# Modulation weights as row pieces with column-tiled products in the mix-in steps of a hybrid retention and convolution network

## What is computed

```python
def adaln(cond, w_ada, b_ada):
    return jnp.split(jax.nn.silu(cond) @ w_ada + b_ada, 6, axis=-1)

# one layer, latent stream
sh1, sc1, g1, sh2, sc2, g2 = adaln(c, w_ada[l], b_ada[l])
p = modulate(x, sh1, sc1) @ w_in[l]                       # modulate: h * (1 + scale) + shift
q, k, v = ...                                             # 8 heads of 64, rotary q and k
o_f, _ = retention_scan(q, k, v, lg_f, s_f)               # chunks of 128, both directions
o_b, _ = retention_scan(flip_seq(q), flip_seq(k), flip_seq(v), lg_b, s_b)
mix_x = mixer_output(o_f + flip_seq(o_b), p, ..., w_out[l])   # gated retention | conv module
x = layer_norm(DEEPNORM_ALPHA * x + g1 * mix_x, ln1_w[l], ln1_b[l])
x = mlp_sublayer(x, sh2, sc2, g2, w_ff1[l], w_ff2[l], ln2_w[l], ln2_b[l])
```

## Time and profile before

| | us |
|---|---|
| three runs | 3217.91, 3218.61, 3223.07 |
| median | 3218.61 |
| profiled execution, its own time | 3222.41 |
| its span in the trace | 3220.6 |
| TensorE busy, and share of the span | 2902.3, 90% |
| VectorE busy, and share of the span | 2237.7, 69% |

### The profile page before, as it was taken

The page is one execution under the profiler, slowest core; times in us unless marked ns, Lnnn a source line. Parts: engine busy times, 40 slices in busy tenths (PEclk is TensorE's granted clock), DMA queues, the critical chain, the costliest instruction groups (busy, mean ns, idle before and its releaser), DMA issues.

```text
span 3220.6 us, 36797 instructions
## 1 busy us (share of the span) xinstructions
PE 2902.3 (90%) x12840; PEld 2268.5 (70%) x12840; DVE 2237.7 (69%) x3490; ACT 709.3 (22%) x1416; POOL 1036.7 (32%) x939
## 2 busy tenths in 40 slices
PE   7798999778699999999997599998797999999994
PEld 1487778347588888888885487784376787777873
DVE  0497675376777786868688787652667778777787
ACT  0322323332311111111111333332323111111111
POOL 0133435165411111111113444462553222222124
PEclk9898999889899999999999799998898999999997
DMA  9311112443011111111112311114421111111111
GB/s 360 73 40 46 48 36 99 138 146 91 26 40 39 39 39 39 39 36 36 35 37 27 104 41 52 56 56 173 132 82 39 53 44 47 46 45 52 39 46 65
DMA packets 256867, 216.06 MB, mean 67 GB/s; under 512 B 60864, under 2 KB 204800, under 8 KB 256768
## 3 DMA queue, kind: packets, MB, share of 16 engines
q10 hardware_dynamic: 143112, 125.89, 12.7%
q1 hardware_dynamic: 113656, 88.93, 9.1%
HBM read 191.62 MB, written 23.17 MB: 67 GB/s over the span
## 4 chain that ended last, share of the span: by engine, by line
PE 75%; DVE 12%; issue 6%; POOL 3%; ACT 2%; DMA 2%; SPq 0%; ACTq 0%; POOLq 0%; DVEq 0%
PE bank L515 12%; PE bank L517 12%; PE bank L516 12%; PE bank L940 8%; PE bank L941 8%; PE bank L942 8%; PE bank L591 5%; PE bank L815 2%; PE bank L816 2%; PE bank L817 2%; DVE work L1565 2%; PE bank L871 1%; PE bank L870 1%; DVE x_hl L1336 1%; PE bank L854 1%
## 5 line engine op out<-in xcount | busy, mean ns | idle before, releaser
L1301 POOL TENSOR_TENSOR w_lo<-raw,w_hi 128x1024 fp32r<-128x1024 f32 x120 | 305.2, 2544 | 1174.8 <-ACT w_hi L1159 1174.8
L1567 DVE TENSOR_TENSOR work<-work 128x512 f32<-128x512 f32 x576 | 555.2, 964 | 20.0
L515 PE MATMUL bank<-w_hi,h_hi 128*128 128x512 f32 x1152 | 458.3, 398 | 43.4 <-DVE work L1565 43.4
L940 PE MATMUL bank<-x_hl,w_hi 128*128 128x512 f32 (+1 forms) x1280 | 474.8, 371 | 2.7 <-ACT work L1150 1.4
L941 PE MATMUL bank<-x_hl,w_hi 128*128 128x512 f32 (+1 forms) x1280 | 472.8, 369 | 0.0
L942 PE MATMUL bank<-x_hl,w_lo 128*128 128x512 f32 (+1 forms) x1280 | 472.3, 369 | 0.0
L517 PE MATMUL bank<-w_hi,h_lo 128*128 128x512 f32 x1152 | 451.7, 392 | 0.0
L516 PE MATMUL bank<-w_lo,h_hi 128*128 128x512 f32 x1152 | 451.5, 392 | 0.0
L1565 DVE TENSOR_TENSOR work<-bank,work 128x512 f32<-128x512 f32 x576 | 393.1, 682 | 0.0
L1466 DVE SCALAR_TENSOR_TENSOR bank<-work,bank 128x512 f32<-128x512 f32 (+1 forms) x580 | 366.5, 696 | 3.9
L1544 DVE TENSOR_TENSOR work<-work 128x512 f32<-128x512 f32 (+1 forms) x160 | 124.9, 781 | 347.3 <-ACT work L1150 347.3
(11 more groups left out here) (131 smaller groups left out, 4451.9 us busy)
## 6 DMA issues: line engine op xcount, KB each, us to landing
raw<-in_w_ff ACTq DMA_DIRECT2D x128, 512.0 KB
plain_words<-in_w_ada SPq DMA_DIRECT2D x12, 2048.0 KB
plain_words<-in_w_ada ACTq DMA_DIRECT2D x12, 2048.0 KB
raw<-in_w_in ACTq DMA_DIRECT2D x64, 256.0 KB
raw<-in_w_in ACTq DMA_DIRECT2D x16, 512.0 KB
raw<-in_w_out ACTq DMA_DIRECT2D x16, 512.0 KB
gate_rows<-work SPq DMA_DIRECT2D x80, 64.0 KB, 1.6
retention_rows<-work SPq DMA_DIRECT2D x72, 64.0 KB, 1.5
```

Of the source, the lines that this page charges most:

```text
L515: nc.tensor.matmul(out_ps, hi, whi, start=first, stop=False)
L940: nc.tensor.matmul(o, slot(mlp_slot(f), 0)[:, wc], x_hi[:, k, cols], start=k == 0, stop=False)
L1301: nc.gpsimd.tensor_tensor(slot(mlp_slot(sl), 1), raw[:, un % 2, :], slot(mlp_slot(sl), 0).bitcast(F32), ALU.subtract).then_inc(w_ready, 1)
L1567: nc.vector.tensor_tensor(X[:, t, hc], X[:, t, hc], y_t[:, yi % 2, :], ALU.add).then_inc(S["y_add"], 1)
```

## The change

The modulation product is cut by rows as well as by columns. A section is one of the 12 vectors of 1024 columns (6 a layer), a piece is 128 rows of it, 512 KB, and eight pieces make a section. For a piece TensorE does four products of 256 columns each, whose outputs stand at partitions 0, 32, 64 and 96 of one bank, so in four column groups of the array. VectorE adds the bias with four instructions of 2 x 256.

- Only sections 0 and 1 precede the first modulate phase: 16 pieces, loaded by SP in four sets, then the tokens in three loads, then the stores of both rows.
- Sections 2 to 7 go with steps 2 to 49 of layer 0's mix-in, and sections 8 to 11 with steps 2 to 33 of layer 1's, one piece a step, at the end of the step's work. There is one piece buffer: SP loads a piece (two transfers of 256 KB) when the products of the one before are done. A section's first product waits until VectorE has added the bias of the section before (`ada_row`), and VectorE does that in the same step, behind its taps.
- Tail and mix-out have no modulation work, and ScalarE issues none of its loads.
- The section's bank is bank 7 (bank 6 for section 1), so the convolution has bank 3 alone: `conv_chain` now does the two latent runs one after the other, and every tap waits for its direct predecessor.
- The modulate phase of both layers transposes into five banks in place of two; in layer 0 ScalarE loads and splits the first four units of projection weights ahead of it, in place of among its steps. The modulation rows are read back ahead of the decay rates.

```diff
-ADA_FIRST, ADA_TAIL = 12, 6
-ADA_LATE = 2
+ADA_FIRST = 2
+ADA_SECTIONS = [list(range(ADA_FIRST, 6 + ADA_FIRST)), list(range(6 + ADA_FIRST, 12))]
+ADA_PIECES_FIRST = ADA_FIRST * KT
...
-    return [(tap, lat + r) for tap in range(TAPS) for r in range(2)] + [(tap, r) for r in range(lat) for tap in range(TAPS)]
+    return [(tap, r) for r in (*range(lat, lat + 2), *range(lat)) for tap in range(TAPS)]
...
             plan.append(("taps", ct, a, b))
             if b < len(chain):
                 taps.insert(0, (ct, b))
+        if stored:
+            plan.append(("ada_bias", stored.pop(0) + 1))
+        if finished:
+            plan.append(("ada_row", finished[0]))
+            stored.append(finished.pop(0))
+        if n >= 2 and pieces:
+            s, k = pieces.pop(0)
+            plan.append(("ada", s, k))
+            if k == KT - 1:
+                finished.append(s)
...
-            return banks[((6, 7), (6, 7, 4, 5))[which][j % (4 if which else 2)]]
+            return banks[((4, 5, 3, 6, 7), (6, 7, 4, 5))[which][j % (4 if which else 5)]]
...
-            for k in range(4 * half, 4 * half + 4):
-                mm = nc.tensor.matmul(ada_bank(g), cond_s[:, k, :], ada_w[g % ADA_BUFS][:, k, :].rearrange("p (a n) -> p a n", a=2),
-                                      start=k == 0, stop=k == KT - 1)
-            if half:
-                mm.then_inc(ada_done, 1)
+            for q in range(4):
+                mm = nc.tensor.matmul(ada_bank(s)[32 * q:32 * q + 2, 0:2 * P], cond_s[:, k, :], columns(q), start=k == 0, stop=k == KT - 1)
+            mm.then_inc(ada_used, 1)
...
+            def ada_piece_load(i):
+                s, k = i // KT, i % KT
+                l, j = s // 6, s % 6
+                for half in range(2):
+                    at = j * D + half * 512
+                    sp.dma_start(ada_half[half], w_ada[l, k * P:(k + 1) * P, at:at + 512]).then_inc(piece_in, 16)
...
+                    if a[0] == "ada":
+                        piece += 1
+                        if piece < KT * (ADA_SECTIONS[l][-1] + 1):
+                            sp.wait_ge(ada_used, piece)
+                            ada_piece_load(piece)
...
                     elif a[0] == "ada":
-                        _, g, half = a
-                        if g % ADA_TAIL == 0 and not half:
-                            pe.wait_ge(S["evac_q"], s0["evac_q"] + NT * PAIRS)
-                        ada_products(pe, g, half)
+                        _, s, k = a
+                        pe.wait_ge(piece_in, 32 * (KT * (s - ADA_FIRST) + k + 1))
+                        if k == 0:
+                            pe.wait_ge(ada_row, s)
+                        ada_products(pe, s, k, lambda q: ada_half[q // 2][:, (q % 2) * 2 * P:(q % 2 + 1) * 2 * P])
...
+                if l == 0:
+                    for u in range(4):
+                        load(l, u)
                 act.wait_ge(S["one_added"], s0["one_added"] + 1)
                 for j in range(N_IN0):
-                    if j % 5 == 0 and j < 20:
+                    if l and j % 5 == 0 and j < 20:
                         load(l, j // 5)
...
-            for g in range(ADA_FIRST):
-                ada_bias(g)
+            def ada_bias(s):
+                dve.wait_ge(ada_used, KT * (s + 1))
+                dve.wait_ge(bias_in, 64 * max(s + 1, ADA_FIRST))
+                for q in range(4):
+                    row = ada_bias_rows(s, q)
+                    last = nc.vector.tensor_tensor(row, ada_bank(s)[32 * q:32 * q + 2, 0:2 * P], row, ALU.add)
+                last.then_inc(ada_row, 1)
...
                             if tap == 0:
-                                if ct or i > 1:
-                                    dve.wait_ge(S["conv_op"], before - (i == 1))
+                                if ct or i:
+                                    dve.wait_ge(S["conv_op"], before)
...
-                                dve.wait_ge(S["conv_op"], before - (1 if r >= lat else 0))
+                                dve.wait_ge(S["conv_op"], before)
```

More of the change, by code:

```diff
@@ L120, in mix_in_plan @@
     n = 0
-    ada = [(g, half) for g in range(ADA_FIRST + ADA_TAIL * layer, ADA_FIRST + ADA_TAIL * (layer + 1) - ADA_LATE) for half in range(2)]
-    rows = []
-    while n < len(steps) or posts or len(valued) < PAIRS * len(tiles) or ada or rows:
+    pieces = [(s, k) for s in ADA_SECTIONS[layer] for k in range(KT)]
+    finished, stored = [], []
+    while n < len(steps) or posts or len(valued) < PAIRS * len(tiles) or pieces or finished or stored:
         if n < len(steps):
@@ L128, in mix_in_plan @@
                     plan.append(("load", loads.pop(0)[0]))
[L129 to L133, removed]
         now = ready[:1] if ready and ready[0] in scored else []
@@ L147, in mix_in_plan @@
                 scored.add(x)
[L148 to L155, removed]
-                if half:
-                    rows.append(g)
             for p, t in now:
@@ L374, in build @@
         ps_sc, ps_o = banks[5][:, 0:2 * P], banks[6]
-        ps_conv = [banks[3], banks[7]]
+        ps_conv, ps_ada = banks[3], banks[7]
         raw_in = [sem(f"raw_in{i}") for i in range(2)]
@@ L569, in beside_ln1, with ada_bank, ada_bias_rows, ada_products @@
             return turns
[L571 to L589, removed]
-            for k in range(4 * half, 4 * half + 4):
-                mm = nc.tensor.matmul(ada_bank(g), cond_s[:, k, :], ada_w[g % ADA_BUFS][:, k, :].rearrange("p (a n) -> p a n", a=2),
-                                      start=k == 0, stop=k == KT - 1)
-            if half:
-                mm.then_inc(ada_done, 1)
+        def ada_bank(s):
+            return banks[6] if s == 1 else ps_ada
+        def ada_bias_rows(s, q):
+            return ada_b[s == 1][32 * q:32 * q + 2, :]
+        def ada_products(pe, s, k, columns):
+            for q in range(4):
+                mm = nc.tensor.matmul(ada_bank(s)[32 * q:32 * q + 2, 0:2 * P], cond_s[:, k, :], columns(q), start=k == 0, stop=k == KT - 1)
+            mm.then_inc(ada_used, 1)
         def cond_of(t):
@@ L773, in _ @@
             pe.wait_ge(cond_ready, 1)
-            for g in range(ADA_FIRST):
-                for half in range(2):
-                    ada_products(pe, g, half)
+            for i in range(ADA_PIECES_FIRST):
+                if i % 4 == 0:
+                    pe.wait_ge(ada_first_in[i // 4], 64)
+                ada_products(pe, i // KT, i % KT, lambda q: ada_first[i][:, q * 2 * P:(q + 1) * 2 * P])
             def transpose_step(l, which, j):
@@ L782, in transpose_step @@
                     ln_source_ready(pe, l, which, t0 + n - 1)
-                nb = 4 if which else 2
+                nb = 4 if which else 5
+                if l == 0 and which == 0 and j == 3:
+                    pe.wait_ge(ada_row, ADA_FIRST)
                 if j >= nb:
@@ L893, in _ @@
                         mm.then_inc(S["cvt_done"], 1)
-                        if st < ADA_LATE:
-                            for half in range(2):
-                                ada_products(pe, ADA_FIRST + ADA_TAIL * (l + 1) - ADA_LATE + st, half)
                     j = st - 3
@@ L1445, in _ @@
                         _, ct, a0, a1 = a
[L1446 removed]
+                        chain = conv_chain(l)
                         if (ct, a0) == (0, 0):
```

109 lines of the change are left out of this document (48 added, 61 removed).

## The result

The changed kernel takes 3233.96 us (median of 5 runs, 3230.95 to 3236.73), the kernel before 3218.23 us in the same comparison (5 runs, 3217.41 to 3223.07). The ratio is 1.0043, with a 95% interval from 1.0032 to 1.0054: slower by 0.4%, clear of the noise. The forecast was 3233.6 us, with a range from 3192 to 3272.

A forecast was written before the change was run, and what follows sets the result against it. TensorE was taken to bound mix-ins and tails, VectorE layer 0's modulate phase, transfers the prologue. 3222.4 (profiled) - 138 + 82.6 + 58.3 + 12 = 3237.4, for the median 3233.6 us; range 3192 to 3272.

The forecast's parts named there:

- Prologue, modulate phase, tails: Time these stages lose: prologue 58 us, modulate phases 11.5 and 3, tails 27 and 34.4 (layer 0, layer 1).
- Mix-outs: Removing matmuls from two mix-out steps gains 4 us (0 to 8), since VectorE's norms hide most of it.
- A piece, 1.12 us: Each mix-in piece costs TensorE five slots of 0.225 us, 1.12 us, as passes of neighbouring column groups overlap.
- The lower bound: Price of a mix-in piece if only its weight loads are paid: 8 x 0.087, 0.70 us.
- a sign of being wrong: In the mix-ins, TensorE hardly waiting for bias rows, or a piece's products overlapping, would make the kernel faster than before.
- that case: Rival: in the mix-ins column groups run fully side by side, 0.70 us a piece, 24 us less, 3209; chance 0.2.
- Drain on a change of tiling mode: The skill's claim that changing tiling mode drains TensorE, here once in and once out a mix-in step; left unpriced.
- Waits for the bias: In both mix-ins TensorE newly waits for bias rows added behind VectorE's taps, 14 us at step 10 of layer 0.
- Taps: Dependent convolution taps of 512 columns in the mix-ins stand 0.80 us apart, 0.14 more than in two banks.
- the cover: In the mix-in of the kernel before, VectorE's lag behind TensorE, 11.6 us at step 10, costs nothing.
- Pieces in transfer: Around step 26 of layer 0's mix-in, SP's piece load queued behind a convolution store adds 2.3 us (0 to 5).
- Cold clock: A slower clock after five long mix-in waits, two in layer 0 and three in layer 1, adds 12 us.

The follow-up runs named there:

- free steps: The changed kernel with one or two steps without a piece after each section: 3194.3 us with one, 3177.43 us with two.
- the other edit: Two steps without a piece after each section of the changed kernel, 3177.43 us; with SP's order changed and early first pieces too, 3152.15 us.

## Why the prediction was right, and where it was not

The time, 3233.6 against 3233.96, is nearer than the working deserves. Inside the two mix-ins two terms were off by more than 20 us each and cancelled. And the working was one for traces: it said 3237.4 for the profiled execution, which took 3230.95, so of the +15 us that it added up the traces show 8.5. That the medians show 15.7 is luck: the trace of before is 3.8 us above its median, as I had allowed for, and that of after is 3.0 below its own.

- **Prologue, modulate phase, tails.** Right, from bytes over the measured rate, and from rows with and without the work. The terms: 60.4 for 58, 12.5 for 11.5, 27.0 for 27, 29.7 for 34.4. The last was mis-sized: in layer 1's tail TensorE now has idle times of 3.48 and 2.40 us at the start and then two iterations of 2.9 us at a lower clock, where I had reckoned 2.05 throughout. The granted clock is 0.61 from 2248 to 2262 us, and was 1.00 from 2228 to 2242, ahead of the idle times. Below, these and then two of the even ones:

```profile
2252.35 0.66 PE L858 MATMUL bank<-work 128*128 128x128 f32 x2 [3.48 <-POOL work L1237]
...
2259.05 1.19 PE L866 MATMUL bank<-work 128*128 128x256 f32 x2 [2.40 <-DVE work L1421]
...
2260.03 0.95 PE L875 MATMUL bank<-work 128*128 128x64 f32 x4
...
2262.88 1.09 PE L875 MATMUL bank<-work 128*128 128x64 f32 x4
...
2265.78 0.63 PE L875 MATMUL bank<-work 128*128 128x64 f32 x4 [0.50 <-DVE work L1432]
...
2267.83 0.63 PE L875 MATMUL bank<-work 128*128 128x64 f32 x4 [0.50 <-DVE work L1432]
```

- **Mix-outs.** I took 4 us. The rows for the whole stretches from a tail's end on give 1.2 together (0.7 lost, 1.9 gained). The products there had been in time for which TensorE now waits: over the whole span its waits at line 914 (912 before) for GpSimd rose from 10.9 to 32.1 us, and those for convolution columns from 46.7 to 55.9.
- **A piece, 1.12 us: wrong.** Measured 0.77. The step that failed is that the second pass of a product must leave a slot of 0.225 us of its own for each group. The lower bound, eight weight loads of 0.087, is what the trace is close to. By 58 pieces this is 20 us too much. The prediction had this as a sign of being wrong (the products of a piece overlap, and the kernel is faster than before); they overlap, and it is slower all the same, since the term of the transfers made up for it. The Trainium skill's rule ("TensorE: Matmul & The Clock Gate", Part 3, Packing small matmuls: matmuls in different column groups run concurrently) agrees with the trace: 2.06 us for one group against 0.77 for four is 2.7 times. I gave that case 0.2.
- **Drain on a change of tiling mode.** The Trainium skill's "TensorEngine Tiling (Array Packing)", Key Properties, has TensorE drained by it. If it is in the 0.77 us, it is small: that number is 0.07 above eight weight loads of 0.087 us.
- **Waits for the bias: right in mechanism, place and size.** Steps 10, 26 and 34 of layer 0: 13.18, 9.90 and 3.27 us (forecast 14, 10.3 and 3); steps 10, 18 and 26 of layer 1: 5.03, 13.36 and 6.75 (6.3 was the forecast for the last). In all 51.5 us, where the forecast's terms without their pieces make some 53. (Its terms for step 18 of layer 1 add up to 14.6, not to the 14.1 that it took.) The runs with free steps and with the bias moved show that these are a loss of their own, worth 38 to 56 us, and not only a place where one is seen.
- **Taps.** 0.79 us apart, against 0.80 forecast, and the cover was rightly named: alone in the kernel before the chain costs nothing that can be told. The cover doesn't hold everywhere: the chain costs 12 us in the runs without pieces.
- **Pieces in transfer: the term that I missed.** I had 2.3 us, it is 24.3, of which 6.2 and 5.1 are at each layer's first piece, which SP issues at the end of the modulate phase. Of the other 13.0, four waits with 10.1 us are for loads that SP issued right behind stores of retention rows or convolution columns, and 2.3 us are at the short context steps, with no store ahead of them. I had looked at the length of a load against a step and not at what stands ahead of it on SP at every retention step, though I had reckoned with just that at step 27.
- **Cold clock: right in sum, not in its parts.** I put 12 us for five waits, 2.5 each. Behind the wait at step 10 of layer 0 the piece takes 1.03 us in place of 0.61, and the next projection starts 0.96 us behind it in place of 0.54. The 24 products of that projection start over 6.83 us (148.54 to 155.37), and over 5.35 in the step before the wait (128.67 to 134.02). That makes 1.9 a wait. But nine of the waits at a piece, not five, are followed by a piece of 1.03 us: five for the bias and four for a transfer, which would be 17 us. The kernel before has slow stretches of its own. Against it the two mix-ins show the 12 us of the ledger, if a piece is 0.77 everywhere.

So 20 us too much for pieces stood against 22 too little for transfers. Counted by stage, the pieces of the two mix-ins were forecast at some 85 us (76 at 1.12 in the terms) and are 62, and 7 us of old waits went, which I had not counted. The mix-ins were 11 us too high with it all, and the other stages, which gained 133.0 us where I had 137.9, 5 us too low. A forecast that hits by that is worth less than its number.

The measured change is +15.7 us in the medians, but +8.5 in the traces. Nothing in the traces explains the difference of 7 us, since each kernel has one trace here; the other executions of after were 2 to 6 us longer than the traced one, and those of before from 5 us shorter to 1 us longer, so it is of the size of that spread.

## What to carry to other kernels

When work is moved under a busy engine, ask of each semaphore that it brings how far behind the engine is that answers it: a lag that cost nothing becomes a stall the moment that somebody waits for something at its end. Here the answer was to ask two steps later, and it was worth 56 us, where the price of the work itself was 20 us off in my prediction. Look at the order of every queue that must deliver something in time, the DMA-issuing one too, and put what is waited for soonest ahead of stores that wait for a slow engine. And take such faults away together: of two waits in one chain, each hides the gain of mending the other (10.7 us alone, 25 on top of the other edit).

## What the runs showed of the hardware

Four 32-bit products with two stationary columns each and 256 moving columns, at four column groups, add 0.77 us to a step, and 2.06 us in one group. In the prologue of after, 16 such products in a row take 2.85 us, 0.71 for four, close to eight weight loads of 0.083 us (the median of the weight loads of line 578). So at this size the weight loads seem to set the pace, and no longer the moving columns; no run here changed the one without the other.

```profile
17.85 2.85 PE L578 MATMUL bank<-plain_words,work 128*2 128x256 f32 x32 [2.45 <-DMA plain_words<-in_w_ada]
...
L578 PEld LDWEIGHTS bank<-plain_words,work x768: 79/83/129, 11.8 to 2086.3; 128*2 128x2 f32 x192
```
